# Conditioning columns from products with ones, and two gate rows made ahead of their residuals

## The reference

```
mod = (silu(c) @ ada_w[layer] + ada_b[layer])[:, None, :]
sh_m, sc_m, g_m, sh_f, sc_f, g_f = split(mod, 6)
h = rmsnorm(x, norm_g[layer, 0]) * (1 + sc_m) + sh_m
y = pool_s5_block(h) if layer == 0 else mamba2_mixer(h)
x = x + g_m * rmsnorm(y, norm_g[layer, 1])
h = rmsnorm(x, norm_g[layer, 2]) * (1 + sc_f) + sh_f
y = swiglu(h) if layer == 0 else moe_swiglu(h)       # top 2 of 8 experts
x = x + g_f * rmsnorm(y, norm_g[layer, 3])
```

## Time and profile before

| | us |
|---|---|
| median of 3 runs | 1679.56 (1677.16 to 1680.3) |
| the profiled execution, its own time | 1678.3 |
| its span in the profile | 1676.2 |
| PE busy | 1544.0 (92%) |
| DVE busy | 429.9 (26%) |
| ACT busy | 215.0 (13%) |
| DMA, mean rate over the span | 290 GB/s |

### The profile page before, as it was taken

How to read it: one execution, slowest core, us unless ns; L and a number is a source line. 1 busy time by engine, 2 the same in 40 slices (tenths; PEclk the granted TensorE clock), 3 DMA queues, 4 the chain that set the end, 5 groups by cost and what they waited for, 6 DMA issues and landing times.

```text
span 1676.2 us, 23905 instructions
## 1 busy us (share of the span) xinstructions
PE 1544.0 (92%) x10681; PEld 906.2 (54%) x10682; DVE 429.9 (26%) x895; ACT 215.0 (13%) x411; POOL 106.1 (6%) x129
## 2 busy tenths in 40 slices
PE   7887999999999999989999998999999889977975
PEld 5644487777588766546343353356666643423322
DVE  6796212232255455222000001010010010100202
ACT  3311300000321143220000000000000000000001
POOL 7164000000000011000000000000000000000000
PEclk9997999999999999998999999999999999999999
DMA  9576386664564403255999986999999969999996
GB/s 339 177 247 236 139 302 244 234 224 169 181 228 151 151 1 143 109 206 216 404 408 409 391 296 259 403 408 408 402 406 395 377 250 404 407 409 403 408 407 240
DMA packets 167297, 485.74 MB, mean 290 GB/s; under 512 B 12928, under 2 KB 15872, under 8 KB 167168
## 3 DMA queue, kind: packets, MB, share of 16 engines
q1 hardware_dynamic: 162624, 482.51, 75.4%
q10 hardware_dynamic: 4544, 1.33, 0.4%
HBM read 482.78 MB, written 1.05 MB: 289 GB/s over the span
## 4 chain that ended last, share of the span: by engine, by line
PE 80%; DMA 8%; DVE 6%; issue 4%; ACT 1%; POOL 0%; DVEq 0%; SPq 0%; POOLq 0%; ACTq 0%
PE bank L1753 26%; PE bank L1280 21%; PE bank L1784 13%; DMA ring<-in_moe_w_down 5%; PE bank L1483 5%; PE bank L1673 3%; DMA ring<-in_moe_w_gate 3%; PE bank L1593 3%; PE bank L1725 2%; PE bank L1287 1%; DVE arena L982 1%; PE bank L1765 1%; PE bank L1632 1%; DVE arena L990 1%; PE bank L1608 1%
## 5 line engine op out<-in xcount | busy, mean ns | idle before, releaser
L1753 PE MATMUL bank<-ring,arena 128*32 128x256 f32 (+3 forms) x3664 | 387.0, 432 | 42.1 <-issue 27.0
L1753 PEld LDWEIGHTS bank<-ring,arena 128*32 128x32 f32 (+1 forms) x3664 | 179.4, 121 | 238.6 <-issue 182.0
L1280 PE MATMUL bank<-arena,ring 128*128 128x256 f32 x1264 | 282.8, 384 | 1.4 <-ACT arena L674 1.0
L1280 PEld LDWEIGHTS bank<-arena,ring 128*128 128x128 f32 x1264 | 240.9, 193 | 34.4 <-ACT arena L674 1.7
L1784 PE MATMUL bank<-ring,arena 128*32 128x256 f32 (+1 forms) x1792 | 208.1, 459 | 16.1 <-DMA ring<-in_moe_w_down 15.3
L1202 DVE TENSOR_TENSOR arena<-arena,bank 128x512 f32<-128x512 f32 (+2 forms) x44 | 24.4, 577 | 658.6 <-PE bank L1753 658.6
L1784 PEld LDWEIGHTS bank<-ring,arena 128*32 128x32 f32 (+1 forms) x1792 | 87.4, 121 | 127.4 <-issue 90.8
L1753 PE MATMUL bank<-arena 128*32 128x256 f32 (+3 forms) x1200 | 116.1, 402 | 9.8 <-issue 4.0
L788 ACT ACTIVATE arena<-bank 128x512 f32<-128x512 f32 (+2 forms) x44 | 21.1, 508 | 645.5 <-PE bank L1765 549.1
L1753 PEld LDWEIGHTS bank<-arena 128*32 128x32 f32 (+1 forms) x1200 | 57.9, 121 | 65.8 <-issue 49.9
L1483 PE MATMUL bank<-ring,arena 128*128 128x512 f32 x176 | 76.9, 595 | 1.5 <-PE bank L1280 1.5
(11 more groups left out here) (274 smaller groups left out, 1240.5 us busy)
## 6 DMA issues: line engine op xcount, KB each, us to landing
ring<-in_moe_w_down SPq DMA_DIRECT2D x46, 2048.0 KB, 19.3
ring<-in_moe_w_up SPq DMA_DIRECT2D x45, 2048.0 KB, 23.6
ring<-in_moe_w_gate SPq DMA_DIRECT2D x41, 2048.0 KB, 23.7
ring<-in_ada_w SPq DMA_DIRECT2D x24, 2048.0 KB, 9.5
arena<-in_moe_w_gate SPq DMA_DIRECT2D x15, 2048.0 KB, 23.6
ring<-in_m_w_in SPq DMA_DIRECT2D x12, 2048.0 KB, 9.0
arena<-in_moe_w_up SPq DMA_DIRECT2D x11, 2048.0 KB, 23.6
arena<-in_moe_w_down SPq DMA_DIRECT2D x10, 2048.0 KB, 21.7
```

The source lines that it names most:

```text
L1280: ins = mm(out_, l, r, start=i == 0, stop=i == len(pairs) - 1, **kw)
L1753: ins = mm(ps[base + b // per][m * h:m * h + m, w * (b % per):w * (b % per) + w], hcur3[:, kc, m * b:m * b + m], sl[:, kc - half * rows, w ...
```

## The change

The four transposes of `ada_turn` become four products of a block with a column of ones. Each adds the block's 128 rows, of which only four are not zero, so that the sum over the parts comes out of PE. Tile `i` now has its own four columns (`4 * i`) of bank 7, and the wait for `mods(i-1)` goes, except before the tiles 12 and 22. The 17 additions on DVE (16 `mods` with two operations each, and one for the tiles 14 to 21) become four of one operation each: tiles 0 to 3, 4 to 11, 12 to 21, 22 and 23. They read bank 7 and the biases. `gg` has two halves, so that `gate_cols` can run one gate ahead. The products for the gate row of residual 2 move from the feed-forward part into norm 2, and those for residual 3 from Mamba's output projection into norm 3, both between `ada_mm` and `turn_x`, with their copies on ACT.

```
-            def mods(i):
-                dve.wait_ge(s["ada_turned"], turn_of(i) + 1)
-                m = modraw[:, i % 2]
-                c.then(v.tensor_reduce(m, bank(7, 4, 4, 32)[:, :, :, 0], AX.X, ALU.add), step)
-                layer, n = i // NADA, i % NADA
-                at = layer * 48 + 4 * n
-                c.inc(tt(mod_flat[:, at:at + 4], m, cols[:, 0, at:at + 4], ALU.add), "mod_ready")
+            def mods(first, last):
+                dve.wait_ge(s["ada_turned"], turn_of(last - 1) + 1)
+                at = slice(4 * first, 4 * last)
+                c.inc(tt(mod_flat[:, at], ps[7][:, at], cols[:, 0, at], ALU.add), "mod_ready")
...
             table_turns(0)
-            mods(0)
-            mods(1)
             table_turns(1)
-            mods(2)
-            mods(3)
+            mods(0, 4)
...
-                if q - 1 in ADA_AT:
-                    mods(ADA_AT[q - 1])
...
             skip(3)
+            mods(4, NADA)
             gate_cols(1, mod[:, 0, 2], norm_col(0, 1))
+            gate_cols(2, mod[:, 0, 5], norm_col(0, 3))
...
             def ada_turn(i):
                 pe.wait_ge(s["ada_copied"], turn_of(i) + 1)
-                if i:
-                    pe.wait_ge(s["mod_ready"], turn_of(i) + (i > NADA + 1))
+                if i in (NADA, 2 * NADA - 2):
+                    pe.wait_ge(s["mod_ready"], 2 if i == NADA else 3)
                 for k in range(4):
-                    ins = turn(ps[7][:, P * k:P * k + P], modparts[i // NADA][:, P * k:P * k + P], ident[:, :])
+                    at = 4 * i + k
+                    ins = mm(ps[7][:, at:at + 1], modparts[i // NADA][:, P * k:P * k + P], ones[:, 0:1], start=True, stop=True)
...
             ada_mm(NADA + 1)
+            pe.wait_ge(s["gg_ready"], 2)
+            pe.wait_ge(s["grow_ready"], 2)
+            row_products(gg[:, 0], 4).then_inc(s["grow_mm"], 1)
             pe.wait_ge(s["x_ready"], 2)
             turn_x(2)
...
-            pe.wait_ge(s["gg_ready"], 2)
-            pe.wait_ge(s["f_act"], 22)
-            row_products(gg, 4).then_inc(s["grow_mm"], 1)
             ffn_down(5)
             ada_mm(2 * NADA - 2)
             ada_turn(2 * NADA - 2)
             ada_mm(2 * NADA - 1)
+            pe.wait_ge(s["gg_ready"], 3)
+            row_products(gg[:, 1], 4).then_inc(s["grow_mm"], 1)
...
-                if t == 2:
-                    pe.wait_ge(s["yT1_a"], 8)
-                    pe.wait_ge(s["yT1_b"], 8)
-                    pe.wait_ge(s["gg_ready"], 3)
-                    row_products(gg, 0).then_inc(s["grow_mm"], 1)
...
 ACT, norm 2 (norm 3 alike, with grow_rows(3, grow1)):
             squares(1)
+            grow_rows(2, grow)
             ada(NADA + 1)
-            hT_high(2, NADA, mod[:, 0, 3])
+            hT_high(2, 2, mod[:, 0, 3])
```

More of the change, by code:

```diff
@@ L81 @@
 ADA = [AT[f"ada{i // NADA}", i % NADA] for i in range(2 * NADA)]
-MODS1 = NADA + 5
+MODS1 = 4
 def turn_of(i):
@@ L140, in hybrid_trunk @@
         mod_flat = mod[:, :, :, :].rearrange("p l v k -> p (l v k)")
-        modraw = sb("modraw", [P, 2, 4])
         cT = sb("cT", [P, KC, 32])
         gs = sb("gs", [P, KC])
-        gg = sb("gg", [P, KC])
+        gg = sb("gg", [P, 2, KC])
         stat = sb("stat", [P, 16])
@@ L633, in _ @@
                 ada(i)
-            hT_high(1, 4, mod[:, 0, 0])
+            hT_high(1, 1, mod[:, 0, 0])
             act.wait_ge(s["turn_ready"], 1)
@@ L708, in _ @@
                     c.inc(f(silu_f[:, n % 2], ps[4][:, 0:TOK], ACT.Silu), "f_silu")
-            grow_rows(2, grow)
             y_squares(2)
@@ L714, in _ @@
             squares(2)
+            grow_rows(3, grow1)
             ada(2 * NADA - 1)
-            hT_high(3, NADA + 3, mod[:, 1, 0])
+            hT_high(3, 3, mod[:, 1, 0])
             act.wait_ge(s["l1_in"], 96)
@@ L869, in gate_cols @@
                 dve.wait_ge(s["mod_ready"], c.n["mod_ready"])
-                if n > 1:
-                    dve.wait_ge(s["grow_mm"], n - 1)
-                c.inc(tt(gg[:, :], gate, g, ALU.mult), "gg_ready")
+                if n > 2:
+                    dve.wait_ge(s["grow_mm"], n - 2)
+                c.inc(tt(gg[:, n % 2], gate, g, ALU.mult), "gg_ready")
             def residual(n, n_sq, n_root, rows_, base=0, prescaled=False):
@@ L1006, in _ @@
             norm_x(2)
-            mods(NADA)
-            scale_cols(2, NADA, mod[:, 0, 4], norm_col(0, 2))
+            scale_cols(2, 2, mod[:, 0, 4], norm_col(0, 2))
             hT_low(2, mod[:, 0, 3])
-            gate_cols(2, mod[:, 0, 5], norm_col(0, 3))
             for t in range(6):
@@ L1022, in _ @@
                         sum_rows(2 * t + j // 2, 4 * (j % 2))
-                if t == 0:
-                    mods(NADA + 1)
             dve.wait_ge(s["tile_used"], AT["ada1", 9] + 1)
-            c.inc(tt(mod_flat[:, 56:88], ps[7][:, 0:32], cols[:, 0, 56:88], ALU.add), "mod_ready")
+            mods(NADA, 2 * NADA - 2)
+            gate_cols(3, mod[:, 1, 2], norm_col(1, 1))
             residual(2, 12, 2, grow)
             norm_x(3)
-            mods(2 * NADA - 2)
-            scale_cols(3, NADA + 3, mod[:, 1, 1], norm_col(1, 0))
+            scale_cols(3, 3, mod[:, 1, 1], norm_col(1, 0))
             hT_low(3, mod[:, 1, 0])
-            mods(2 * NADA - 1)
-            gate_cols(3, mod[:, 1, 2], norm_col(1, 1))
+            mods(2 * NADA - 2, 2 * NADA)
             dve.wait_ge(s["l1_in"], 96)
@@ L1340, in _ @@
             pe.wait_ge(s["c_ready"], 1)
+            pe.wait_ge(s["consts"], 9)
             for i in range(3):
@@ L1357, in _ @@
                     if m == 1:
-                        pe.wait_ge(s["mod_ready"], 4)
+                        pe.wait_ge(s["mod_ready"], 1)
                         pe.wait_ge(s["bx_ready"], 8)
@@ L1471, in ada_columns @@
                 for k in range(4):
-                    at = 4 * (n - 2) + k
+                    at = 4 * (NADA + n) + k
                     ins = mm(ps[7][:, at:at + 1], modsum[:, n % 2, P * k:P * k + P], ones[:, 0:1], start=True, stop=True)
@@ L1545, in turn_conv @@
                         .then_inc(s["b_turned1"], 1)
-            pe.wait_ge(s["grow_ready"], 4)
+            pe.wait_ge(s["grow_ready"], 6)
             for n in range(32):
@@ L1695, in _ @@
             pe.wait_ge(s["gg_ready"], 4)
-            row_products(gg, 6).then_inc(s["grow_mm"], 1)
+            row_products(gg[:, 0], 6).then_inc(s["grow_mm"], 1)
             pe.wait_ge(s["mask_ready"], 1)
```

8 lines of the change are left out of this document (2 added, 6 removed).

## The result

| | before | after |
|---|---|---|
| median, runs | 1678.87 (1676.82 to 1681.11), 20 | 1682.97 (1677.83 to 1689.61), 20 |
| ratio, 95% interval | | 1.0031 (1.0021 to 1.0041) |
| the profiled execution, its own time | 1678.3 | 1685.43 |
| its span | 1676.2 | 1683.7 |

The kernel became slower by 4.1 us where I had forecast 2.8 us less. The time is outside my range. I had given 0.09 to a slower kernel, mostly for another reason (the clock in the norms), which did not come. The numbers are of executions in the usual state; one of experiment 10 took 2306.91 us at a granted clock of 0.65 and is not in its ratio.

What follows compares the result with a forecast made beforehand. PE, with 80% of the chain of waits, was taken as the bound. Terms -0.4 - 1.97 + 1.4 - 1.78 + 0.3 + 1.4 - 1.78 gave -2.8 us: 1676.5 us predicted, range 1672.5 to 1680.5.

Steps and rivals of the forecast that it cites:

- the clock falls in the norms: Rival: PE's clock drops in norms 2 and 3, costing each 5.0 us; +7.2 in all, 1686.8 us; chance 0.08.
- The carry to the end: From the edits, all before 742 us, to the end: their summed shifts move the end one to one, -2.8 us.
- Head: Conditioning tiles at the start: PE's second turn no longer waits 1.5 us for DVE; -0.4 us, bounds -1.6 and +0.4.
- S5 loop: Loop paced by DVE: without `mods` ten steps take 51.3 against 53.27 us; -1.97 us, bounds 0 and -2.6.
- Norms 2 and 3: Gate products added ahead of the transposes make PE later; +1.4 us in each norm, bounds +1.1 and +3.2.
- Feed-forward part: Gate products before the last `ffn_down` go, -1.78 us; `ada_turn(13)` between full PE work costs +0.3.
- Mamba: Gate products between the output tiles of Mamba's projection go; -1.78 us.
- the clock stays up: Rival: PE keeps full clock behind the loop and norm 3, gaining 5.1 us more; -7.9, 1671.6 us; chance 0.09.
- Sum up to norm 4: All terms, from edits before 742 us, add to -2.8 us, so the first expert starts 2.8 us earlier.
- the norms give it all back: Rival: `hT_high` on ACT comes 1.1 us late in norms 2 and 3; sum -0.6, 1679.0 us; chance 0.18.

Runs made afterwards that it cites:

- experiment 10: Kernel before with six more warming products behind the first conditioning tile in the head; 1678.83 us, ratio 0.9997.
- exp. 12: Changed kernel with its head's warming products split 12, 3 and 3 in place of 6, 6 and 6, no later instruction moved; 1684.19 us, ratio 1.0023.
- exp. 5: Changed kernel with two more TensorE instructions (waits long reached) ahead of the first gather; 1673.26 us, ratio 0.9969.
- experiment 6: Kernel before with 112 more TensorE instructions that wait for nothing, ahead of the turn of `C`; 1703.80 us, ratio 1.0155.
- 7: Kernel before with 114 more TensorE instructions that wait for nothing, ahead of the turn of `C`; 1691.37 us, ratio 1.0084.
- experiment 1: The changed kernel run again with no edit; 1683.22 us, ratio 1.0029 against the kernel before.
- experiment 2: Changed kernel with only the turns (products with ones, four additions), the gate rows made where they were before; 1673.65 us, ratio 0.9971.
- experiment 4: Changed kernel with 12 in place of 6 warming products behind the first conditioning tile in the head; 1672.31 us, ratio 0.9967.
- 11: Changed kernel with six more warming products in the head and two more instructions ahead of the first gather; 1673.86 us, ratio 0.9964.
- experiment 3: Kernel before with only the gate rows moved into norms 2 and 3, transposes and DVE operations kept; 1671.74 us, ratio 0.9954.
- experiment 8: Kernel before with 96 more TensorE instructions that wait for nothing, ahead of the turn of `C`; 1700.60 us, ratio 1.0125.
- experiment 9: Kernel before with two more TensorE instructions (waits long reached) ahead of the first gather; 1677.98 us, ratio 0.9996.

## Why the prediction was wrong, point by point

Times in the profiles at the same places. The last row is the median of the runs.

| start of | before | after | exp. 12 | exp. 5 |
|---|---|---|---|---|
| first input product | 39.26 | 43.02 | 39.13 | 39.51 |
| the loop's L982 that waits 2.83 us for PE | 82.30 | 84.88 | 82.61 | 81.36 |
| end of the loop's last sum | 150.10 | 150.74 | 148.48 | 147.20 |
| `ada_mm(12)` | 197.46 | 198.34 | 195.56 | 194.41 |
| feed-forward products | 205.85 | 208.40 | 205.63 | 204.48 |
| `ada_mm(22)` | 446.06 | 447.18 | 444.40 | 443.25 |
| Mamba's products | 455.04 | 457.80 | 455.03 | 453.88 |
| norm 4's warming products | 741.96 | 741.16 | 738.40 | 737.22 |
| first expert | 778.63 | 779.44 | 773.22 | 771.40 |
| second expert | 860.66 | 867.16 | 860.98 | 853.41 |
| third expert | 1022.22 | 1031.24 | 1029.03 | 1014.84 |
| span | 1676.2 | 1683.7 | 1683.8 | 1669.8 |
| median | 1678.87 | 1682.97 | 1684.19 | 1673.26 |

- **The carry to the end: the step that failed.** "All edits lie before 742 us, so I add up the shifts of their places and carry the sum to the end." An edit also moves every later instruction of its engine in the stream. Here it moved them by 112, and the branch into the second expert landed on the last instruction of a piece, as I read it from the single weight load. That costs 5.7 us there and 1.1 us or more at the third expert. Experiment 5 against the changed kernel, and 6 against 7, differ by two idle instructions alone and show it. My evidence for "A microsecond won or lost before then moves the end by a microsecond" was a stretch from 1050 us on; the two branches that cost lie at 858 and 1025 us, and the pauses put down to "issue" were no term of my sum. In the profiles the loss adds up so: 0.8 us at the first expert, 5.7 to the second, 2.5 to the third (1.1 in the pause, 1.4 in the 128 products at a lower clock), and 1.5 given back from there to the end, 7.5 in all. This profile lies above the median of its runs; that of experiment 1, at 1682.21, shows the same two pauses.
- **Head: -0.4 forecast, +2.6 found at the loop (-0.9 in experiments 2 and 5).** The wait for DVE did go. The turn took 1.05 at full clock with its first load and 1.86 at half, against my 1.2, and the clock stayed low. The same code in experiments 2 and 5 had the third tile at 28.7 and the loop a microsecond earlier than before (81.36): a low clock in the head is something that this code has in some executions. With more warming products all the tiles took 1.92 us in 4 and 11. Experiment 12 shows that it does not decide the result.
- **S5 loop: right.** -1.94 (65.86 against 67.80 from the second to the third row of the table), forecast -1.97.
- **Norms 2 and 3: right.** +1.67 for norm 2 with `ada_turn(12)` (10.06 against 8.39), +1.64 for norm 3 (10.62 against 8.98), forecast +1.4 each, the turn included. The gate products took 1.89 to the start of the transposes and these 1.91, against my 1.78 and 1.7. The turns alone cost 0.30 and 0.01 (experiment 2), the rows alone 1.28 and 1.25 (experiment 3).
- **Feed-forward part: nearly right.** -1.43 (238.78 against 240.21), forecast -1.78 + 0.3 = -1.48.
- **Mamba: the mechanism right, the size off.** -3.56 (283.36 against 286.92), forecast -1.78. The rest is the slow stretch behind norm 3, which is gone in all profiles of kernels with both parts (283.3 to 283.4 us, six profiles) and stays with either part alone (286.71 and 284.91 us). I would have booked it as a piece of the rival "the clock stays up", but experiment 6, whose Mamba part is that of the kernel before, took 283.48 us, and experiment 8 took 285.13. So the fall of the clock can go when the same work merely comes at another time. Whether the edit or the time took it away here is not shown: experiments 7, 9 and 10, also with the Mamba part of before, kept it (286.8 to 287.0 us). Behind the loop the clock still fell: 9.39 us for 32 of L1268 at 159 us, against 9.12. The Trainium skill ("TensorE: Matmul & The Clock Gate", Part 4: PE-mode transpose) says that transposes do not count as work for the clock as products do; the products with ones did not keep it up here.
- **Sum up to norm 4.** At 742 us after was 0.8 us ahead with its slow head, and experiment 5, with a fast one, 4.7. Without the 1.7 us of the fall of the clock in Mamba that is 3.0, beside the forecast of 2.8. The rivals "the norms give it all back" and "the clock falls in the norms" did not happen; the granted clock was 1.00 from 196 to 212 us and from 445 to 460. But norm 4, which is not in my sum, took 1.6 us more at a lower clock, so that the first expert came 0.8 us late and not 2.8 early.

Both parts with a good landing are faster than before: 1673.26 (experiment 5) and 1672.31 (experiment 4), as is the rows-only kernel with 1671.74. Which of these is the fastest the intervals do not tell.

Open: why executions of the changed kernel spread over 12 us (five of the 20 took over 1688 us) where those before spread over 4; the 12.4 against 5.6 us of experiments 6 and 7; why the same code from the third expert to the sixth took between 342.8 us (experiment 1) and 352.3 (experiment 8), though the traces show other pauses there (16.9 against 21.6 us) and more time at the lower clock (4.9 against 17.8 us); and the rows-only kernel's gain of 5.4 us between the fourth expert and the end (564.3 against 569.7 us), where the kernel before with two instructions more had none.

## What to carry to other kernels

Where a long program has data-dependent branches, an edit anywhere ahead of them can change the pause at a branch by where it lands, here by up to 5.7 us; it need not (experiment 9). Before you believe a result within 0.5%, compare the pauses put down to "issue" before and after, and run the same kernel with a few idle instructions more. Here two of them were worth more than the change itself.

## What the runs showed of the hardware

TensorE's instructions come in packets of 16 KB on a queue of their own (q8: 106 packets, 1.74 MB in the kernel after). In the stage with small products the pauses show how much is in one. Timeline of the kernel after, fifth expert:

```profile
1337.16 3.70 PE L1738 MATMUL bank<-ring,arena 128*32 128x128 f32 x128 [1.69 <-issue]
1343.37 0.96 PE L1738 MATMUL bank<-ring,arena 128*32 128x128 f32 x26 [2.51 <-issue]
```

Exactly 128 products with their 128 weight loads run in 3.70 us, and then PE waits 2.51: 256 instructions in each 6.2 us, so here the supply of instructions is what bounds PE. The Trainium skill says the same of the size ("Advanced Engine Details and Errata", ISA Cache: 16 KB, 256 instructions, two lines), and that a taken branch out of the present window stalls for a fetch ("Runtime: NRT & Kernel Launch", Instruction fetch mechanics). The trace agrees. The same section calls the crossing of a 16 KB boundary mostly hidden; here it is not, at 3.70 us of work to 6.2 us of supply. In these runs the branch into the second expert cost 3.1 to 3.2 us with a piece's start or middle as its target. The next piece was asked for 5.8 to 5.9 us after the first though the queue was idle; at the third expert it was asked for after 3.1 to 4.6, and what sets this is open. At the second expert a landing with one instruction left in its piece cost 8.8 us, with 17 left 3.2 and then 3.6.

A wait on TensorE whose count is long reached is not free: 112 instructions with two such waits each took 11.8 us, and 96 took 10.1.
